# Sums of h made in the up stage, another order of DVE's work in the down stage, and another beginning of both feed-forwards in a Strassen encoder layer

## The reference

```
x = x + 0.5 * swiglu(rmsnorm(x), w1_gate, w1_up, w1_down)      # first feed-forward, width 2816
x = x + token_mix(rmsnorm(x))                                  # SSD, gated linear and softmax attention
x = x + 0.5 * swiglu(rmsnorm(x), w2_gate, w2_up, w2_down)      # second feed-forward
swiglu(h) = (silu(h @ w_gate) * (h @ w_up)) @ w_down
```

## Time and profile before

| | |
|---|---|
| median of 3 runs | 2301.75 us (2301.37 to 2306.05) |
| profiled execution | 2299.27 us, span of its instructions 2297.5 us |
| PE, weight loads | busy 2112.5 us (92%), 2022.1 us (88%) |
| DVE, ACT, POOL | busy 1242.8, 780.5, 319.1 us |
| DMA | 270.05 MB, mean 118 GB/s |
| mean granted clock of PE | 0.962 |

### The profile page before, as it was taken

How to read it: one execution, slowest core, us unless ns; L and a number is a source line. 1 busy time by engine, 2 the same in 40 slices (tenths; PEclk the granted TensorE clock), 3 DMA queues, 4 the chain that set the end, 5 groups by cost and what they waited for, 6 DMA issues and landing times.

```text
span 2297.5 us, 36074 instructions
## 1 busy us (share of the span) xinstructions
PE 2112.5 (92%) x15227; PEld 2022.1 (88%) x15227; DVE 1242.8 (54%) x1750; ACT 780.5 (34%) x1223; POOL 319.1 (14%) x423
## 2 busy tenths in 40 slices
...
GB/s 135 57 67 85 75 85 67 82 122 292 259 257 217 228 84 123 59 1 38 20 39 38 42 1 124 112 32 85 75 79 73 75 85 92 220 267 234 232 236 208
DMA packets 58752, 270.05 MB, mean 118 GB/s; under 512 B 6568, under 2 KB 11016, under 8 KB 49248
## 3 DMA queue, kind: packets, MB, share of 16 engines
...
## 4 chain that ended last, share of the span: by engine, by line
PE 69%; DVE 12%; DMA 11%; issue 4%; POOL 3%; ACT 1%; SPq 0%; ACTq 0%; POOLq 0%; DVEq 0%
PE ps L165 61%; DMA sb_h_raw<-h_kept 10%; DVE sb_down_lo L738 2%; DVE sb_h_lo L807 2%; POOL sb_h_raw L761 2%; PE ps L1144 2%; PE ps L1183 2%; DVE sb_h_raw L780 2%; PE ps L1156 1%; DVE sb_nrm L272 1%; PE ps L209 1%; POOL sb_rms L185 1%; DVE sb_x L384 1%; DMA sb_h_first_raw<-h_kept 1%; DVE sb_seg L1828 1%
## 5 line engine op out<-in xcount | busy, mean ns | idle before, releaser
L165 PE MATMUL ps<-sb_xh,sb_up_hi 128*128 128x272 f32 x2480 | 720.2, 290 | 32.0 <-ACT sb_t L530 17.0
L165 PE MATMUL ps<-sb_xl,sb_up_hi 128*128 128x272 f32 x2480 | 719.7, 290 | 0.0
L165 PE MATMUL ps<-sb_xh,sb_up_lo 128*128 128x272 f32 x2480 | 719.2, 290 | 0.0
L165 PEld LDWEIGHTS ps<-sb_xh,sb_up_hi 128*128 128x128 f32 x2480 | 472.1, 190 | 38.6 <-issue 26.7
L165 PEld LDWEIGHTS ps<-sb_xh,sb_up_lo 128*128 128x128 f32 x2480 | 471.7, 190 | 0.0
L165 PEld LDWEIGHTS ps<-sb_xl,sb_up_hi 128*128 128x128 f32 x2480 | 471.5, 190 | 0.0
L165 PE MATMUL ps<-sb_h_hi,sb_down_hi 128*128 128x272 f32 x1188 | 359.4, 302 | 95.3 <-DVE sb_down_lo L738 95.3
L165 PE MATMUL ps<-sb_h_hi,sb_down_lo 128*128 128x272 f32 x1188 | 355.8, 299 | 0.0
L165 PE MATMUL ps<-sb_h_lo,sb_down_hi 128*128 128x272 f32 x1188 | 355.7, 299 | 0.0
L165 PEld LDWEIGHTS ps<-sb_h_hi,sb_down_hi 128*128 128x128 f32 x1188 | 237.7, 200 | 101.4 <-DVE sb_down_lo L738 101.4
L165 PE MATMUL ps<-sb_nh,sb_whi 128*128 128x362 f32 (+1 forms) x696 | 233.0, 335 | 6.4 <-ACT sb_fq L991 4.4
...
## 6 DMA issues: line engine op xcount, KB each, us to landing
sb_down_raw<-wb SPq DMA_DIRECT2D x92, 704.0 KB, 5.1
sb_h_raw<-h_kept POOLq DMA_DIRECT2D x110, 544.0 KB, 6.5
...
h_kept<-sb_hbuf POOLq DMA_DIRECT2D x42, 544.0 KB, 2.9
...
sb_h_first_raw<-h_kept POOLq DMA_DIRECT2D x10, 544.0 KB, 5.1
...
```

Source lines behind the costliest of these rows:

```text
L165: mm = K.nc.tensor.matmul(out, a, b, start=first and n == 0, stop=last and n == 2, skip_group_check=loose)
```

## The change

- *h sums.* h tiles are taken in pairs (even and odd column tile), which are the two halves of the down product's inner dimension; the down weights are laid out for that on the host. After every second column tile `h_sums` makes the five sums and differences that the passes use, on VectorE, and POOL stores all seven operands to a new `h_kept`. A pass then loads one operand, in chunks of 4352 bytes a partition, into three buffers in turn; `chunk_sum` is gone. The last tile of pass 0 is split from SBUF, without a load.
- *Order.* In `down_dve` `down_lo` comes before the chunk splits, and `down_sum` after them for the group after next; the first updates come later. The weight halves go into five single buffers. `down_hi` of group 0 and the splits of chunks 0 to 2 come one product later.
- *Beginning.* Ones and gains are loaded before x. VectorE squares the second quarter; the squares of the third and fourth are added on POOL, and PE sums each with one matmul. `up_first_pe` makes gate and up item by item, four banks side by side. T3 and T4 are made and split after P1 and P2 of column tile 1.
- *x back.* Before the second feed-forward x is reloaded on SP's queue instead of POOL's.

The core of the diff. Semaphore counts, addresses and unchanged helpers are left out, and so are removed lines, which stand in the functions printed above:

```diff
 DOWN = (
+    (((1, 1, 0), (1, 1, 1)), 0, ((1, 1, 0), (-1, 1, 1))),
+    (((1, 1, 0), (-1, 0, 0)), 5, ((1, 1, 1),)),
+    (((1, 0, 0),), 3, ((1, 0, 1), (1, 1, 1))),
+    (((1, 0, 0), (1, 1, 1)), 2, ((1, 0, 0), (1, 1, 1))),
+    (((1, 1, 1),), 4, ((1, 0, 0), (1, 1, 0))),
+    (((1, 0, 0), (1, 0, 1)), 1, ((-1, 0, 0), (1, 0, 1))),
+    (((1, 0, 1), (-1, 1, 1)), 6, ((1, 0, 0),)),
 )
+H_SUMS = (((0, 0), (1, 1), ALU.add), ((0, 1), (1, 1), ALU.subtract), ((1, 0), (0, 0), ALU.subtract),
+          ((0, 0), (0, 1), ALU.add), ((1, 0), (1, 1), ALU.add))
...
+def first_sum_pool(K, e, N):
+    for c in (2, 3):
+        for k in range(1, KT):
+            n = (KT - 1) * (c - 2) + k
+            e.wait_ge(N.f.sq, N.was.sq + KT * (c - 1) + k + 1)
+            if k > 1:
+                e.wait_ge(N.f.added, N.was.added + n - 1)
+            K.nc.gpsimd.tensor_tensor(first_square(K, c, 0), first_square(K, c, 0), first_square(K, c, k),
+                                      ALU.add).then_inc(N.f.added, 1)
...
+def first_square_dve(K, e, N):
+    a, b = QUARTERS[1]
+    e.wait_ge(K.x_in[1], 16)
     for k in range(KT):
+        K.nc.vector.tensor_tensor(first_square(K, 1, k), K.x[:, k, a:b], K.x[:, k, a:b], ALU.mult)\
+            .then_inc(N.f.sq_dve, 1)
...
+    for k in range(KT):
+        square(0, k)
+    rstd_act(K, e, N, 0, QUARTERS[0], KT, 4)
     for n in range(FIRST):
         up_hi(K, e, N, n)
+    rstd_act(K, e, N, 1, QUARTERS[1], 2 * KT, 5)
...
+    for tau in range(2):
+        if tau:
             if between:
                 between()
             e.wait_ge(N.f.rstd, N.was.rstd + rstds[1])
+        for k in range(KT):
+            e.wait_ge(N.f.xlo, N.was.xlo + KT * tau + k + 1)
+            for m in range(2):
+                if k % 4 == 0:
+                    e.wait_ge(N.f.alo, N.was.alo + 2 * m + k // 4 + 1)
+                for h in range(2):
+                    bank = (4, 6, 2, 0)[2 * tau + m] + h
+                    q, kk, slot = ITEM_AT[2 * tau + k // 4], k % 4, 2 * m + k // 4
+                    cols, w = slice(Q * h, Q * h + Q), slice(P * kk, P * kk + P)
+                    mm = three(K, K.ps[:, bank, :Q], K.ahi[:, slot, w], K.alo[:, slot, w],
+                               K.xh[:, q, kk, cols], K.xl[:, q, kk, cols], k == 0, k == KT - 1, loose=True)
+                if k == KT - 1:
+                    mm.then_inc(N.f.prod, 1)
...
+    xsum_hi(K, e, N, X_T2, 0)
     up_hi(K, e, N, 4)
     up_hi(K, e, N, 5)
+    xsum_hi(K, e, N, X_T2, 1)
     e.wait_ge(N.f.prod, N.was.prod + 3)
     silu(K, e, N, pair(K.g2_first), bank2(K, 2))
     xsum_hi(K, e, N, X_T1, 0)
     xsum_hi(K, e, N, X_T1, 1)
+    up_hi(K, e, N, 6)
     up_hi(K, e, N, 7)
...
+        if c == 1 and q in (P1, P2):
+            xsum_hi(K, e, N, {P1: X_T3, P2: X_T4}[q], 0)
+            xsum_hi(K, e, N, {P1: X_T3, P2: X_T4}[q], 1)
         if c == FT - 1:
+            if q == P5:
                 down_hi(K, e, N, 0)
+            for ch in {P5: (0,), P7: (1, 2), P3: (3,), P4: (4, 5)}.get(q, ()):
...
+def h_sums(K, e, N, j):
+    e.wait_ge(N.f.h, N.was.h + 4 * j + 4)
+    if j == 0:
+        e.wait_ge(N.f.xlo, N.was.xlo + 2 * KT + 8)
+    elif j == KF - 1:
+        e.wait_ge(N.f.summed, N.was.summed + 3 * (FT - 1))
+    else:
+        e.wait_ge(N.f.hss, N.was.hss + 32 * j)
+    for q, (a, b, op) in enumerate(H_SUMS):
+        K.nc.vector.tensor_tensor(h_stage(K, j, q), h_block(K, j, *a), h_block(K, j, *b), op)\
+            .then_inc(N.f.hsum, 1)
...
 def up_start_dve(K, e, N):
     xsum_dve(K, e, N, X_T1, 0)
     xsum_dve(K, e, N, X_T1, 1)
     xsum_dve(K, e, N, X_T2, 0)
     xsum_dve(K, e, N, X_T2, 1)
+    up_lo(K, e, N, 4)
+    gated(K, e, N, 0, 0)
+    up_sum(K, e, N, 1, 0)
+    up_lo(K, e, N, 5)
     xsum_lo(K, e, N, X_T2, 0)
     xsum_lo(K, e, N, X_T2, 1)
+    up_sum(K, e, N, 1, 1)
+    xsum_lo(K, e, N, X_T1, 0)
+    up_lo(K, e, N, 6)
+    xsum_lo(K, e, N, X_T1, 1)
     gated(K, e, N, 0, 1)
     up_lo(K, e, N, 7)
     xsum_dve(K, e, N, X_T3, 0)
     xsum_dve(K, e, N, X_T3, 1)
+    up_sum(K, e, N, 1, 2)
+    up_sum(K, e, N, 1, 3)
...
+            if c % 2 and c < FT - 1:
+                h_sums(K, e, N, c // 2)
...
+        if c == 1 and q == P1:
+            xsum_lo(K, e, N, X_T3, 0)
+            xsum_lo(K, e, N, X_T3, 1)
+            xsum_dve(K, e, N, X_T4, 0)
+            xsum_dve(K, e, N, X_T4, 1)
+        if c == 1 and q == P2:
+            xsum_lo(K, e, N, X_T4, 0)
+            xsum_lo(K, e, N, X_T4, 1)
         if c == FT - 1:
+            if q == P6:
                 down_sum(K, e, N, 0)
+            elif q == P5:
                 down_lo(K, e, N, 0)
+            for ch in {P5: (0,), P7: (1, 2), P3: (3,), P4: (4, 5)}.get(q, ()):
                 chunk_lo(K, e, N, ch)
+            if q == P4:
+                down_sum(K, e, N, 1)
+                h_sums(K, e, N, KF - 1)
...
+    def store(j):
+        e.wait_ge(N.f.h, N.was.h + 4 * j + 1)
+        e.dma_start(hs[0, :, j], h_block(K, j, 0, 0)).then_inc(N.f.hst[0], 16)
+        e.wait_ge(N.f.h, N.was.h + 4 * j + 4)
+        e.dma_start(hs[1, :, j], h_block(K, j, 1, 1)).then_inc(N.f.hst[1], 16)
+        e.wait_ge(N.f.hsum, N.was.hsum + 5 * j + 5)
+        a, b = (K.hs_a_last, K.hs_b_last) if j == KF - 1 else (K.hs_a, K.hs_b)
+        e.dma_start(hs[2:4, :, j].rearrange("i p t -> p i t"), a[:]).then_inc(N.f.hss, 16)
+        e.dma_start(hs[4:7, :, j].rearrange("i p t -> p i t"), b[:]).then_inc(N.f.hss, 16)
+    for j in range(KF - 1):
+        store(j)
+    e.wait_ge(N.f.hst[0], N.was.hst[0] + 16 * (KF - 1))
+    e.wait_ge(N.f.hss, N.was.hss + 32 * (KF - 1))
+    for n in range(NCH - 1):
+        if n > 1:
+            e.wait_ge(N.f.hclo, N.was.hclo + n - 1)
+        chunk_load(K, e, N, hs, n)
+    store(KF - 1)
     e.wait_ge(N.f.hclo, N.was.hclo + NCH)
+    e.wait_ge(N.f.hss, N.was.hss + 32 * KF)
+    e.wait_ge(N.f.hst[0], N.was.hst[0] + 16 * KF)
+    e.wait_ge(N.f.hst[1], N.was.hst[1] + 16 * KF)
     e.dma_start(K.x[:, 4:8], x_src[:, 4:8]).then_inc(N.f.xl[1], 16)
...
+    e.wait_ge(N.f.hss, N.was.hss + 32 * (KF - 1))
+    for t in range(len(DOWN[0][0])):
+        load(0, t, N.f.bwe)
+    for m, (g, t) in enumerate(TERMS):
+        if m == 0:
+            e.wait_ge(N.f.alo, N.was.alo + PRODUCTS)
+        elif m == 2:
+            e.wait_ge(N.f.prod, N.was.prod + PRODUCTS)
+        elif m >= RAWS:
+            e.wait_ge(N.f.blo, N.was.blo + TERMS[m - RAWS][0] + 1)
+        load(g, t, N.f.bw[m % RAWS])
...
+UPDATED_AT = [()] * 3 + [(0,), (1, 2), (3, 4)] + [(g - 1,) for g in range(6, GROUPS)]
 def down_dve(K, e, N, last=None):
     for g in range(GROUPS):
         p, d = divmod(g, 4)
+        for u in UPDATED_AT[g]:
+            down_update(K, e, N, u)
         if g + 1 < GROUPS:
             down_lo(K, e, N, g + 1)
+        if p + 1 < NP:
+            for ch in CHUNKS_AT[d]:
+                chunk_lo(K, e, N, NCH * (p + 1) + ch)
+        if g + 2 < GROUPS:
+            down_sum(K, e, N, g + 2)
...
+        if n < NCH + STAGES:
+            e.wait_ge(N.f.prod, N.was.prod + PRODUCTS)
+        else:
+            e.wait_ge(N.f.hclo, N.was.hclo + n - STAGES + 1)
+        chunk_load(K, e, N, hs, n)
+        if n == NCH + STAGES - 1:
             e.wait_ge(N.f.grp, N.was.grp + 1)
             e.dma_start(K.x[:, 0:4], x_src[:, 0:4]).then_inc(N.f.xl[0], 16)
...
+            sp.dma_start(K.ones, i["const"][:, C_ONE:C_ONE + P]).then_inc(K.ones_in, 16)
+            sp.dma_start(K.vec[:], i["vec"]).then_inc(K.ones_in, 16)
             for c, (a, b) in enumerate(QUARTERS[:2]):
                 sp.dma_start(K.x[:, :, a:b], x_in[:, :, a:b]).then_inc(K.x_in[c], 16)
...
+                if s == BASE_OUT + 2:
+                    sp.wait_ge(M.x_out, 16)
+                    sp.wait_ge(M.y2, NTT)
+                    for t in range(OUT_STEPS):
+                        sp.dma_start(K.x[:, 2 * t:2 * t + 2], o["x_kept"][:, 2 * t:2 * t + 2]).then_inc(K.x_in[t], 16)
...
-        return down.reshape(2, KF, P, KT, P).transpose(0, 3, 2, 1, 4).reshape(2, KT, P, BW)
+        return down.reshape(KF, 2, P, KT, P).transpose(1, 3, 2, 0, 4).reshape(2, KT, P, BW)
...
-    outs["h_kept"] = nc.dram_tensor("h_kept", (FT, P, T), F32, kind="Internal").ap()
+    outs["h_kept"] = nc.dram_tensor("h_kept", (NP, P, KF, HALF), F32, kind="Internal").ap()
```

More of the change, by code:

```diff
@@ L294, in product_at @@
     return (1 + (n - FIRST) // 7, (n - FIRST) % 7)
-def loads_of(values):
-    return sum(16 * v for v in values)
 def up_weight(K, n):
@@ L800, in chunk_hi @@
         e.wait_ge(N.f.grp, N.was.grp + 4 * (p - 1))
[L801 removed]
+    K.nc.scalar.copy(K.hbh[p % 2][:, chunk_at(n)], chunk_raw(K, n)).then_inc(N.f.hchi, 1)
 def chunk_lo(K, e, N, n):
@@ L862, in down_dve @@
         p, d = divmod(g, 4)
-        if g:
-            down_update(K, e, N, g - 1)
-        if g + 1 < GROUPS:
-            down_sum(K, e, N, g + 1)
-        chunks = [NCH * (p + 1) + ch for ch in CHUNKS_AT[d]] if p + 1 < NP else []
-        for n in chunks:
-            chunk_sum(K, e, N, n)
```

(16 more changed lines are left out.)

238 lines of the change are left out of this document (84 added, 154 removed), and 7 rows, old and new, of the table DOWN.

## The result

The changed kernel takes **2201.53 us** (median of 4 runs, 2200.73 to 2205.18) against 2302.36 (4 runs of the kernel before beside it): a ratio of 0.9562, interval 0.9546 to 0.9579. It is 101 us faster; 2194 was predicted, with a range of 2178 to 2220. The profiled execution took 2202.06 us (span 2200.3), 97.2 less than the one of before.

What follows compares the result with a forecast made beforehand. PE was held in the down stages, 148 us lost, mostly waiting for DVE's down_lo behind loads. Terms sum to 107.5 us off 2299.27, giving 2191.8; with 2.5 added for the median, 2194, range 2178 to 2220.

Steps and rivals of the forecast that it cites:

- groups 4 to 27, first and second: Down stage from group 4 on, in both feed-forwards: 24 groups at 8.38 us, 41.6 and 44.2 us less.
- opening, first and second: Start of each down stage, up to group 4: group 1 earlier, then a wait before group 2; 3.7 and 7.2 us less.
- beginning of the first feed-forward: First items start earlier, then slow beside POOL's additions; the 8.5 us wait moves to P7; 6.8 us less.
- beginning of the second: Start of the second feed-forward, without squares or POOL additions: gate and up together, 4 us less, bounds 0 and 8.
- The mechanism: Down stage: down_lo waited behind loads and chunk sums on DVE; no chunk sums, fewer loads, earlier weight sum would free it.
- The slow clock after the wait: Opening of the down stage, group 2: PE restarts at half clock after idling, costing some 2.5 us.
- The prediction's own sign of error: Opening of the down stage: the forecast would be wrong if stores of the last sums landed later than 6 us.
- Sums in the up stage: Up stage: five extra DVE operations every 42 us cost nothing; without cover, up to 3 us per pair, 60 in all.
- The rule that spoke against it: POOL's h loads and stores: DMA issues can be held while DVE locks the shared port pair; up to 2220, chance 0.03.
- The longer opening: Rival for the down stage's opening: queued landings 6 us later, twice, or a half-clock start; 20 us more, 2214, chance 0.13.
- Waits in the steady passes: Rival from group 4 on: ACT's in-order list keeps half of the 86 us gained; 2237, chance 0.10.
- the landing of 18 us: Rival, slower than before: three chunk buffers turn too slowly, a landing of 18.1 us would eat 107 us; chance 0.04.

## Why the prediction was right, and where it was not

The parts, from the traces of before and after; the terms sum to 97.2 against 107.5.

| Term | predicted less | measured less |
|---|---|---|
| groups 4 to 27, first and second | 41.6, 44.2 | 43.4, 46.0 |
| opening, first and second | 3.7, 7.2 | -4.2, 0.3 |
| beginning of the first feed-forward | 6.8 | 7.4 |
| beginning of the second | 4 | 4.3 |

**Groups 4 to 27.** Size right: 8.30 us a group, 0.08 under the 8.38 of the earlier trace rows. Of the 89 us, 63 were idle time of PE; the other 26 lie in its busy time, 212.2 and 212.7 us at a granted clock of 0.95 and 0.94 against 199.3 at 1.00. The mechanism was right in its core (a wait for a load ahead of `down_lo`) and too wide in its list. Neither DVE's load nor the traffic nor the weight sum's place was needed for it; two of the conditions of before together, two buffers and an operation that waits ahead of `down_lo`, bring back 32 us. In the kernel before, the chain that ended last runs through the same round, with two loads to a sum (start us, length us, what):

```profile
595.31 2.16 POOL sb_h_raw L761 x3
597.47 7.73 DMA sb_h_raw<-h_kept
605.23 1.29 DVE sb_h_raw L780
606.52 1.20 DVE sb_down_lo L738
607.97 1.29 DVE sb_h_lo L807
609.27 0.29 issue
609.56 0.72 POOL sb_h_raw L761
```

From issue to issue that is 14.25 us. The weight sum is 1.3% of that chain from 582 to 824. That the round with its second load and the weight sum make up the other 57 of the 89 us is argued, not shown: that combination was not run.

**Opening: the term that was mis-sized, by 7.9 and 6.9 us.** The chain was named rightly, in its order: chunk 4, sums, stores, x and chunks, then group 2's weight sum behind the splits; PE waited there and nowhere later. Two landings were too short: chunk 4's, taken at the median of the earlier trace rows, and the stores', taken at 4.3 "beside weights". With three weight halves in flight chunk 4 took 9.4 us, with two more the stores took 9.1; the split of chunk 4 came 3.7 us late by this, the landing of the stores 8.2. The other landings came near what was put: chunk 2 took 3.8, 5.2 predicted, and the three chunks of pass 1 landed 9.7 to 12.3 us after x's issue, 11 predicted. So from the last up product group 1 started at 22.0 instead of 18.2, group 2 at 48.9 instead of 40.2, group 4 at 67.4 instead of 59.5. The slow clock after the wait was about right: group 2 took 10.2 us at a granted clock of 0.80, 1.9 over 8.30, and 2.5 were put. The prediction's own sign of error, stores later than 6 us, is what came.

**Beginnings.** Items started at 18.2, not 16.2, as ACT's second root waited for PE's sums of the squares, which ended at 17.1. They went quicker (17.5 us for eight instead of 20.3), and the second half started at 40.1, 40.6 predicted: two misses that nearly cancel, so that this agreement is in part luck. (From 44.62 to 40.6 is 4.0, not the 4.1 of the prediction's sum.) An item beside POOL took 2.42 us, 2.5 predicted. The wait moved from P6 to P7 as worked out.

**Sums in the up stage** cost nothing: from 90.5 to 495 PE has no gap in the trace after, with DVE's 234 us in 404.5.

**The rule that spoke against it.** All 82 issues of h chunks took 0.53 to 0.57 us; 50 of them had DVE at work for over 90% of their time and took 0.53 in the mean, 27 for under 10% and took 0.54. No run here shows POOL's DMA issues held up by DVE.

**The rivals.** The longer opening had the right direction, and 15 of its 20 us. Waits in the steady passes and the landing of 18 us did not come.
